# Three of five decay masks made ahead in GpSimd's order, and the next head's products in fewer, longer runs on TensorE

## What is computed

```python
gc = jnp.cumsum(to_chunks(g), axis=-1)
diff = gc[..., :, None] - gc[..., None, :]
decay = jnp.where(incl, jnp.exp(jnp.where(incl, diff, 0.0)), 0.0)
a_mat = jnp.where(strict, bc[..., :, None] * kk * decay, 0.0)
sol = triangular_solve(a_mat, rhs, left_side=True, lower=True, unit_diagonal=True)
def step(s, xs):
    v_new = u_i - w_i @ s
    o_i = qg_i @ s + qk_i @ v_new
    s = s * gl_i + kd_i.T @ v_new
```

## Time and profile before

| | |
|---|---|
| median of three runs | 2733.16 us |
| the profiled execution's own time | 2735.79 us |
| its span | 2734.0 us |
| first to last start of a head's preparation, heads 0 to 7 | 712.8 to 1632.2 us |
| preparation of heads 0 to 7, TensorE's first product to P(0) | 32.2, 29.7, 31.3, 31.3, 29.7, 29.7, 31.2, 26.5 us |
| inversion of head 5, P(0) to the residual | 25.3 us |

### The profile page before, as it was taken

How to read it: one execution, slowest core, us unless ns; L and a number is a source line. 1 busy time by engine, 2 the same in 40 slices (tenths; PEclk the granted TensorE clock), 3 DMA queues, 4 the chain that set the end, 5 groups by cost and what they waited for, 6 DMA issues and landing times. The chain is left out here.

```text
span 2734.0 us, 40299 instructions
## 1 busy us (share of the span) xinstructions
PE 2547.3 (93%) x16246; PEld 2120.3 (78%) x16246; DVE 1404.5 (51%) x2110; ACT 808.6 (30%) x1745; POOL 866.0 (32%) x580
## 2 busy tenths in 40 slices
PE   6999999999898989898989898999999999998999
PEld 4768887888687868686868787787778888886887
DVE  5783664114355555554646464335775555555242
ACT  4223553101254444445444444311121111112010
POOL 1443652332313132323222222234633333331121
PEclk9999999997899999999999999999999999999999
DMA  7222232231000000000000000232431111112443
GB/s 266 72 67 86 109 116 77 70 107 40 9 17 32 9 32 9 32 9 32 9 32 25 16 24 17 88 105 93 139 119 47 55 47 47 48 48 87 126 134 94
DMA packets 52646, 177.01 MB, mean 65 GB/s; under 512 B 5360, under 2 KB 14960, under 8 KB 51184
## 3 DMA queue, kind: packets, MB, share of 16 engines
q1 hardware_dynamic: 50160, 170.24, 19.3%
q10 hardware_dynamic: 2304, 4.20, 0.4%
HBM read 148.20 MB, written 20.97 MB: 62 GB/s over the span
## 5 line engine op out<-in xcount | busy, mean ns | idle before, releaser
L201 PE MATMUL late_ps<-h_hi,late_w_hi 128*128 128x512 f32 x784 | 305.6, 390 | 5.9 <-ACTq L127 3.2
L203 PE MATMUL late_ps<-h_hi,late_w_lo 128*128 128x512 f32 x784 | 305.0, 389 | 0.0
L202 PE MATMUL late_ps<-h_lo,late_w_hi 128*128 128x512 f32 x784 | 305.0, 389 | 0.0
L1403 PE MATMUL late_ps<-h_hi,dn_w_hi 128*128 128x512 f32 (+1 forms) x640 | 252.5, 394 | 5.6 <-issue 5.6
L1403 PE MATMUL late_ps<-h_lo,dn_w_hi 128*128 128x512 f32 (+1 forms) x640 | 254.9, 398 | 0.0
L1403 PE MATMUL late_ps<-h_hi,dn_w_lo 128*128 128x512 f32 (+1 forms) x640 | 253.1, 395 | 0.0
L184 POOL CAST late_w_hi<-late_w_raw 128x1024 fp32r<-128x1024 f32 x76 | 79.4, 1045 | 501.7 <-issue 376.0
L191 POOL TENSOR_TENSOR late_w_lo<-late_w_raw,late_w_hi 128x1024 fp32r<-128x1024 f32 x76 | 204.0, 2684 | 6.1
L2444 DVE SCALAR_TENSOR_TENSOR ffn_u<-ffn_pad,vectors,ffn_u 128x1024 f32<-128x1024 f32 x88 | 194.5, 2210 | 3.1
L201 PEld LDWEIGHTS late_ps<-h_hi,late_w_hi 128*128 128x128 f32 x784 | 147.2, 188 | 37.4 <-issue 6.7
L202 PEld LDWEIGHTS late_ps<-h_lo,late_w_hi 128*128 128x128 f32 x784 | 147.2, 188 | 30.7 <-issue 0.2
(11 more groups left out here) (360 smaller groups left out, 6117.5 us busy)
## 6 DMA issues: line engine op xcount, KB each, us to landing
late_w_raw<-in_w_up SPq DMA_DIRECT2D x44, 512.0 KB, 3.5
down_w_raw<-in_w_down SPq DMA_DIRECT2D x32, 704.0 KB, 4.4
late_w_ada<-in_w_ada SPq DMA_DIRECT2D x8, 2048.0 KB, 8.3
dn_w_raw<-in_w_dn SPq DMA_DIRECT2D x32, 512.0 KB, 3.8
w_ada<-in_w_ada SPq DMA_DIRECT2D x8, 1024.0 KB, 11.1
at_w_raw<-in_w_mg_at SPq DMA_DIRECT2D x16, 512.0 KB, 4.0
late_w_raw<-in_w_mg_dn SPq DMA_DIRECT2D x16, 512.0 KB, 3.7
late_w_raw<-in_w_out SPq DMA_DIRECT2D x16, 512.0 KB, 3.8
```

What stands on the lines that cost most here:

```text
L201: pe.matmul(out, self.hi[j][:, k, :], xh, start=(k == 0), stop=False)
L202: pe.matmul(out, self.hi[j][:, k, :], xl, start=False, stop=False)
L203: mm = pe.matmul(out, self.lo[j][:, k, :], xh, start=False, stop=(k == self.kt - 1))
L1403: mm = pe.matmul(bank[at_bank(s)][:, 0:n], wt[:, k, :], x[:, k, t0:t0 + n], start=(rest == 0), stop=(rest == GROUP_MM - 1))
```

## The change

`masked_g(2)` and `masked_g(3)` are issued ahead of `units()`, and `masked_g(4)` behind the first `affine_select`; their waits are unchanged. In the inversion a run has 4 products and stands in substeps 4, 8, ..., 28: 7 runs with the same 28 products. In the chain the rooms become 1.7, 1.8 and 0 in every step, with slot 1 of step 4 at 0 as before. The planner then gives: 14+9, 7+8, 8+7, 8+8, 7+0, 8+7, 8+8, 9+15, 10+8, 7+8 in slots 0 and 1, and none in slot 2; the taps stay where they were, and one evacuation moves from step 1 to step 2. No instruction is added or removed.

```diff
-PREP_FILL, INV_FILL, INV_FROM, ENTRY_FILL, TAIL_FILL = 4, 2, 4, 8, 20
+PREP_FILL, INV_FILL, INV_FROM, INV_EVERY, ENTRY_FILL, TAIL_FILL = 4, 4, 4, 4, 8, 20
 def chain_fill():
-    room = [[1.15, 1.6, 0.75] for _ in range(NCH)]
-    room[Q_SUM_STEP][2] = room[K_SUM_STEP][1] = 0
-    for r in range(3):
-        room[SPREAD_STEP + r][2] = 0.35
+    room = [[1.7, 1.8, 0] for _ in range(NCH)]
+    room[K_SUM_STEP][1] = 0
     room = [r for step in room for r in step]
-    first = BT * PREP_FILL + (STEPS + 4 - INV_FROM) // 2 * INV_FILL + ENTRY_FILL
+    first = BT * PREP_FILL + (STEPS + 4 - INV_FROM) // INV_EVERY * INV_FILL + ENTRY_FILL
...
             for n in range(STEPS + 3):
                 if n < STEPS:
                     p(n)
-                if fill and n >= INV_FROM and n % 2 == 0:
+                if fill and n >= INV_FROM and n % INV_EVERY == 0:
                     pe_fill(pe, h + 1, at, at + INV_FILL)
                     at += INV_FILL
...
-            for bt in range(2):
+            for bt in range(4):
                 masked_g(bt)
             units()
             for bt in range(BT):
...
-                if bt + 2 < BT:
-                    masked_g(bt + 2)
+                if bt == 0:
+                    masked_g(4)
```

## The result

The changed kernel takes 2630.94 us (median of 4 runs, 2628.85 to 2633.85) against 2733.24 (4 runs, 2729.6 to 2743.19): a ratio of 0.962, 95% interval 0.959 to 0.965, so 102 us less. The forecast was 2623, with 2602 to 2648 as its range.

What follows compares the result with a forecast made beforehand. TensorE was taken to be held up in the preparations by waits for GpSimd's masked g and the clock lost with them. 2735.8 - 122.3 + 7.7 + 4.2 = 2625.4, less 2.6 for the median: 2623 us, range 2602 to 2648.

Steps and rivals of the forecast that it cites:

- part one: Preparations, masks issued earlier on GpSimd: 15.3 us each, 12.2 in the last head, 119.3 in place of 241.6, so -122.3 us.
- The ring: Preparations: masked g, VectorE's products and TensorE's k k wait on each other through three engines, TensorE idle 3.25 us each turn.
- Part two: Inversion, runs of four for pairs: +1.1 us a head, +7.7 in all; ends -0.75 to +1.6 a head.
- A change of kind: TensorE going over from small matmuls to next-head products and back: 0.11 us in the inversion, nothing extra in the chain.
- Part three: Chain, slot 2 left without runs: cover lost behind KV in two steps, net +0.6 us a head, +4.2 in all.
- the signs: What would show it right: preparations about 15 us, inversions 26 to 27, KS 0.8 behind KV, chains near 59.3.
- The sum: Whole kernel: 2735.8 - 122.3 + 7.7 + 4.2 = 2625.4 us, forecast as 2623 for the median.
- rival B: The clock still falls, once in each preparation (1.7 us) and in five more chains (1.6 each): 2645 us; chance 0.22.
- A: Longer runs pay, with no new wait in inversion or chain: 2606 us; chance 0.12.
- C: GpSimd is late for decay 4 in the preparations, 4.85 us staying in each head: 2662 us; chance 0.07.
- E: The early masks wait for decays that come too late, so the change doesn't do what it says: 2745 us; chance 0.01.
- D: Thin stretches of chain steps 2 and 4 each set off a long low clock, 168 us in all: 2791 us; chance 0.02.

Runs made afterwards that it cites:

- the one-by-one run: Masks moved, chain's plan of before, the inversion's 28 products in runs of 1 in each of substeps 3 to 30; 2618.69 us (median of 2 runs).
- The two versions with products at the entry: Masks moved, chain's plan and pairs of before, four products moved from preparation's first step to inversion's entry: 2609.97 us; with sums of k also halved: 2606.89 us.
- the units first: Masks 2 and 3 behind units() in place of ahead of it, else as the kernel before with only the masks moved; 2614.22 us (median of 2 runs).
- Y ahead of X: Masks moved, chain's plan of before, fours in the inversion, Y(n-3) ahead of X(n-1) on TensorE and ScalarE; 2619.97 us (median of 2 runs).

## Why the prediction was right, and what was off

**What bounds the kernel, and part one.** Right. The ring was broken, the preparation became what TensorE's list costs (15.3 forecast, 15.0 found; 12.2 and 12.0 in the last head), and the sum of -122.3 stands against -124.9 in the span. The schedule for GpSimd was right to a few tenths, but for `masked_g(4)`, which ended at 5.9 where 6.7 was the latest; the units ended at 4.3, inside 4.0 to 5.0. The rest beyond the waits was clock, as said: all the new preparations run at 1.00.

**Part two.** Mechanism right, size off: 1.5 a head in place of 1.1, within its ends. The period of four was 3.59 (1336.76 to 1340.35), just above the 3.50 to 3.57 that was worked out, and the periods cost the 0.9 that was taken for them. The term for the end of the inversion was the one mis-sized: I took 0.2 for the run that hid the wait before Y(27), and from P(27) to the residual it is 3.31 us in place of 2.75, 0.56 more. The wait itself, in head 5:

```profile
1349.98 0.31 PE L1555 MATMUL late_ps<-identity_half,x_half 128*128 128x64 f16 x5 [0.65 <-ACT y_half L1801]
```

Head 0's inversion lost another 1.4 to the clock.

**A change of kind.** In the inversion the one-by-one run measured 0.11 for it. In the chain no price was found: KS(1) and KS(2) stand 0.77 and 0.83 behind KV where 0.44 is the cost of KV itself, 0.72 a head for the missing cover, and the net loss is 0.7, so leaving nine runs out gained nothing that the numbers show. By the page of the Trainium skill that the prediction cites ("TensorE: Matmul & The Clock Gate", "Step-by-step: what each phase is for") it would have been free in both; the chain agrees with that, the inversion does not.

**Part three.** Right in kind and size: KS(1) stands 0.77 behind KV(0) (0.76 was taken from the last head), with the wait for the state at both steps, and the net is 0.7 a head (0.6 forecast). The chain by itself takes 60.1, not the "near 59.3" of the signs: the three products of slot 2 of step 9 now stand ahead of the last OQ, which takes 0.7 from the head's end into the chain. The rows:

```profile
1243.39 0.61 PE L1659 MATMUL dn_bank<-r_and_v,kv_tok 128*128 128x128 f32 x4
1244.16 0.71 PE L1645 MATMUL dn_bank<-state,k_t 128*128 128x128 f32 x4 [0.16 <-DVE state L1937]
```

**The sum** came out 8 us low. Nearly half of it is 3.7 us before the DeltaNet stage. The other is falls of the clock: rival B's mechanism, in part. Four chains had one in place of two (3.2 us), and head 0's inversion (1.4); B's falls in the preparations did not come. That nothing else is left is partly luck: the preparations came out 2.6 us better than the sum, and the inversions and chains, at full clock, 2.9 worse. The rule of the Trainium skill that stands beside B did not show here: the waits of 0.2 us for the mask in the inversions of heads 1 to 6 left the clock at 1.00. Outside the last head, an inversion has a fall in eight cases in the profiles, with fours, pairs and sevens alike. Each begins 2.4 to 3.1 us behind P(0), where TensorE has just waited 1.05 us ahead of P(2) and waits 0.36 ahead of P(4). The two versions with products at the entry have none there.

**Rivals** A, C and E fell: with the masks alone the time was lower still (A), no wait before decay 4 remained (C), and the preparations halved (E). D was not seen; no chain took over 61.7. But half the change by itself was slower, by 36 us: 15 by the small terms of parts two and three, and most of the rest by falls of the clock.

## What to carry to other kernels

An engine's hand-written order should let a producer run as soon as its own input and its buffer are free, not behind a wait that has nothing to do with it: three instructions moved were worth 120 us, because the wait closed a ring through three engines and the idle stretches also cost TensorE its clock. Background work on TensorE is best cut into runs that each cover one round trip of the foreground to another engine, and no finer: an inversion took 25.1 us with pairs, 26.6 with fours and sevens, and 26.0 with single products, where each further change of kind costs 0.11. When a change has several parts, run each alone: here one part gave 120 us and two together took 16 back.

## What the runs showed of the hardware beyond that

VectorE's output norm, with both inputs in SBUF, took 2.97 us beside GpSimd's copies and 1.22 in the changed kernel, where they come later:

```profile
1362.48 2.97 DVE L1993 TENSOR_TENSOR o_normed<-o_acc,o_stats 128x1024 f32<-128x1024 f32 x1
...
1304.11 1.22 DVE L1991 TENSOR_TENSOR o_normed<-o_acc,o_stats 128x1024 f32<-128x1024 f32 x1
```

With the units first it was 2.98 again, and the second copy 3.32 in place of 2.32: the two engines hold each other up there. By the earlier trace rows they seem to take turns: the norm begins inside the first copy and ends at 1365.45, 1.1 behind that copy's end, and the second copy is 1.0 longer than alone. It was hidden in all versions.

The granted clock falls just after the sums of k, in some chains and not in others of the same list; each fall costs 1.6 us. In the fourteen profiles 41 of the 98 chains of heads 0 to 6 have one, and each begins 0.1 to 1.5 us behind the last of these one-column matmuls. In the kernel before, TensorE was busy for 60.3 of 60.3 us in such a chain, so no idle stretch is needed for it. In the run without the masks, where heads 1 to 6 had one length, it came in each of them; in the changed kernel with three runs a step it came in none, though two inversions had one; with Y ahead of X, the same fours and the same plan, it came in three. What decides between one chain and the next is not shown. A difference of up to 10 us between two versions can come from this alone.
